# Half-height score matmuls in a two-layer hybrid kernel: 64 contracted rows per component instead of 128 with zeroed copies

## The reference, cut to what matters

```python
# branch A: a head's score is a 128-wide part plus a 64-wide rotary part (kr is shared by all heads)
sc = (einsum('bqhd,bkhd->bhqk', qn_b, kn) + einsum('bqhr,bkr->bhqk', qr_b, kr)) * scale   # 128 and 64 wide
# branch B: each head has two components (c = 0, 1) of width 64, with a softmax each
sc = einsum('bqhcd,bkhcd->bhcqk', q_b, k_b) * scale
p = softmax(where(mask, sc, -inf))
a = p[:, :, 0] - lam * p[:, :, 1]
# branch C: one 128-wide score per head, plus a bias
```

## Time and profile before

| | |
|---|---|
| median of 3 runs | 3480.88 us |
| the profiled execution | 3482.22 us |
| its span, first to last instruction | 3480.6 us |
| mean granted TensorE clock | 0.995 of full speed |
| matmul instructions | 28014 |
| DMA from and to memory | 584.18 MB, mean 168 GB/s |

### The profile page before, as it was taken

The page is one execution under the profiler, slowest core; times in us unless marked ns, Lnnn a source line. Parts: engine busy times, 40 slices in busy tenths (PEclk is TensorE's granted clock), DMA queues, the critical chain, the costliest instruction groups (busy, mean ns, idle before and its releaser), DMA issues. The chain is left out here.

```text
span 3480.6 us, 73373 instructions
## 1 busy us (share of the span) xinstructions
PE 3400.6 (98%) x28014; PEld 3325.1 (96%) x28014; DVE 2156.6 (62%) x3522; ACT 1701.2 (49%) x2781; POOL 184.6 (5%) x208
## 2 busy tenths in 40 slices
PE   7889999999999999999999999999999999999999
PEld 7888999999999998999999999999899999999999
DVE  6666756656656665667655665555667655565554
ACT  5444744434434454655544554444655554554443
POOL 1000000000000024000000100000000000000000
PEclk9999999999999999999999999999999999999999
DMA  4223555555555554344455445554344355444554
GB/s 178 97 96 115 174 181 187 195 184 183 192 181 193 184 178 155 134 151 151 149 195 185 177 156 187 187 188 172 131 152 152 142 180 200 174 160 181 182 188 169
DMA packets 90612, 584.18 MB, mean 168 GB/s; under 512 B 10480, under 2 KB 11120, under 8 KB 28400
## 3 DMA queue, kind: packets, MB, share of 16 engines
q1 hardware_dynamic: 88992, 577.60, 47.1%
q0 software_dynamic: 1488, 4.72, 0.4%
HBM read 580.19 MB, written 2.10 MB: 167 GB/s over the span
## 5 line engine op out<-in xcount | busy, mean ns | idle before, releaser
L185 PE MATMUL bank<-h,w_hi 128*128 128x256 f32 x5760 | 1640.2, 285 | 20.6 <-DVE w_lo L166 11.0
L166 DVE TENSOR_TENSOR w_lo<-raw,w_hi 128x768 fp32r<-128x768 f32 (+5 forms) x1202 | 1348.6, 1131 | 475.9 <-ACT w_hi L161 472.5
L186 PE MATMUL bank<-h,w_hi 128*128 128x256 f32 x5760 | 1611.6, 280 | 0.0
L187 PE MATMUL bank<-h,w_lo 128*128 128x256 f32 x5760 | 1610.1, 280 | 0.0
L161 ACT ACTIVATE w_hi<-raw 128x768 fp32r<-128x768 f32 (+5 forms) x1202 | 1105.8, 968 | 242.4 <-PE bank L187 225.9
L185 PEld LDWEIGHTS bank<-h,w_hi 128*128 128x128 f32 x5760 | 1086.1, 189 | 35.5 <-DVE w_lo L166 10.9
L186 PEld LDWEIGHTS bank<-h,w_hi 128*128 128x128 f32 x5760 | 1086.6, 189 | 2.8 <-issue 1.4
L187 PEld LDWEIGHTS bank<-h,w_lo 128*128 128x128 f32 x5760 | 1086.0, 189 | 0.0
L185 PE MATMUL bank<-mixed,w_hi 128*128 128x256 f32 x2368 | 666.4, 281 | 10.2 <-issue 5.8
L186 PE MATMUL bank<-mixed,w_hi 128*128 128x256 f32 x2368 | 663.4, 280 | 0.0
L187 PE MATMUL bank<-mixed,w_lo 128*128 128x256 f32 x2368 | 662.4, 280 | 0.0
(11 more groups left out here) (369 smaller groups left out, 2646.8 us busy)
## 6 DMA issues: line engine op xcount, KB each, us to landing
raw<-in_w SPq DMA_DIRECT2D x485, 1024.0 KB, 4.8
raw<-in_w_br SPq DMA_DIRECT2D x96, 512.0 KB, 4.2
raw<-in_w_uq SPq DMA_DIRECT2D x8, 768.0 KB, 4.3
raw<-in_w_ukv SPq DMA_DIRECT2D x8, 512.0 KB, 3.3
bias_t<-in_bias POOLq DMA_DIRECT2D x16, 192.0 KB, 3.2
x<-in_x SPq DMA_DIRECT2D x4, 512.0 KB, 7.9
raw<-in_w_kr SPq DMA_DIRECT2D x4, 512.0 KB, 3.3
out_x<-x SPq DMA_DIRECT2D x3, 512.0 KB, 7.8
```

Source lines behind the costliest of these rows:

```text
L166: dve.tensor_tensor(w_lo[:, b % 2, c], raw[:, b, c], w_hi[:, b % 2, c].bitcast(F32), ALU.subtract).then_inc(S["lo_done"], 1)
L185: pe.matmul(o, w_hi[:, b % 2, c], a_hi, start=start and k == t0, stop=False)
L186: pe.matmul(o, w_hi[:, b % 2, c], a_lo, start=False, stop=False)
L187: last = pe.matmul(o, w_lo[:, b % 2, c], a_hi, start=False, stop=stop and k == t0 + nt - 1)
```

## The change

The two half-empty copies go. The query of both components (branch B), and of both heads of a pair (branch A), lies in slot 0 alone, on its own half of the partitions. The score matmuls of branch B contract over 64 rows each, partitions 0 to 63 or 64 to 127, with the components alternating within a block: component 0 into `m[3]`, component 1 into `m[4]`, then the second block of each. The rotary matmul of branch A also contracts over the head's own 64 rows, between the 128-row matmuls of the first part. The POOL memset and its semaphore go; DVE's adds become one of 128 x 512 in `rotate` and one of 128 x 256 in `pair_rope`.

```diff
+HALVES = (slice(0, 64), slice(64, P))
...
-            pool.memset(qk[:, 0:2, :], 0.0).then_inc(S["qk_zero"], 1)
...
                 if br == BR_B:
-                    act.wait_ge(S["b_rope"], 3 * B)
+                    act.wait_ge(S["b_rope"], B)
...
-                for k, r in enumerate((slice(0, 64), slice(64, P))):
-                    dve.tensor_tensor(qk[r, k, :], rope[r, 0, :], rs[r, 0, :], ALU.add).then_inc(S["b_rope"], 1)
-                dve.tensor_tensor(qk[:, 2, :], rope[:, 1, :], rs[:, 1, :], ALU.add).then_inc(S["b_rope"], 1)
+                dve.tensor_tensor(qk[:, 0:3:2, :], rope, rs, ALU.add).then_inc(S["b_rope"], 1)
...
-                dve.wait_ge(S["qk_zero"], 1)
...
-                for k, r in enumerate((slice(0, 64), slice(64, P))):
-                    dve.tensor_tensor(qk[r, k, :], rope[r, 0, :], rope[r, 1, :], ALU.add).then_inc(S["qr_rope"], 1)
+                dve.tensor_tensor(qk[:, 0, :], rope[:, 0, :], rope[:, 1, :], ALU.add).then_inc(S["qr_rope"], 1)
...
-                    pe.wait_ge(S["b_rope"], 3 * B + 3)
+                    pe.wait_ge(S["b_rope"], B + 1)
                 else:
                     pe.wait_ge(S["qk_n"], 2 * T + 2)
-                for c in range(2 if br == BR_B else 1):
-                    q = qk[:, c if br == BR_B else 3, :]
+                if br == BR_B:
                     for k, (a, b) in enumerate(((0, P), (P, 3 * P))):
                         tok = slice(k * P, (k + 1) * P)
-                        mm = pe.matmul(m[3 + c][:, a:b], q[:, tok], qk[:, 2, 0:b - a], start=True, stop=br != BR_A)
-                        if br == BR_A:
-                            mm = pe.matmul(m[3 + c][:, a:b], qk[:, e, tok], kr[:, 0:b - a], start=False, stop=True)
-                    mm.then_inc(S[f"score{c}"], 1)
+                        for c, r in enumerate(HALVES):
+                            mm = pe.matmul(m[3 + c][:, a:b], qk[r, 0, tok], qk[r, 2, 0:b - a], start=True, stop=True)
+                            if k == 1:
+                                mm.then_inc(S[f"score{c}"], 1)
+                    return
+                r = HALVES[e]
+                for k, (a, b) in enumerate(((0, P), (P, 3 * P))):
+                    tok = slice(k * P, (k + 1) * P)
+                    mm = pe.matmul(m[3][:, a:b], qk[:, 3, tok], qk[:, 2, 0:b - a], start=True, stop=br != BR_A)
+                    if br == BR_A:
+                        mm = pe.matmul(m[3][:, a:b], qk[r, 0, tok], kr[r, 0:b - a], start=False, stop=True)
+                mm.then_inc(S["score0"], 1)
...
-                    pe.wait_ge(S["qr_rope"], 2 * pair + 2)
+                    pe.wait_ge(S["qr_rope"], pair + 1)
```

## The result

The changed kernel takes 3490.01 us (median of 18 runs, 3486.98 to 3502.4) against 3481.28 us (18 runs, 3477.05 to 3490.36): the ratio is 1.0028, with a 95% interval of 1.0019 to 1.0037. In a later comparison it took 3488.4 us (12 runs) against 3481.41, ratio 1.0014 (1.0006 to 1.0023). It is slower, by some 0.2%. The timed executions of both kernels fall into a faster group of 11 (3477 to 3483 before, 3486 to 3491 after) and a slower one of 7 (from 3485.6 and from 3495.0), and the medians of the two faster groups differ by 8.7 us as well.

A forecast was written before the change was run, and what follows sets the result against it. PE was taken to bound the kernel, busy 98% of the span. Terms +10.2 + 5.1 - 3.5 - 1.3 = +10.5 us on the median 3480.9 gave 3491.4 us; range 3478 to 3506, the forecast's own 3486 to 3497.

The forecast's parts named there:

- A trip into half height and back, 0.32: PE's score matmuls: going to half height and back costs 0.32 us, bounds 0 and 0.55.
- The hold: At a height change on PE, the weight load waits until the matmul ahead is nearly out: 0.206 or 0.31 us.
- the matmul follows its load by about 0.03: Going down to half height on PE, the matmul starts about 0.03 us after its load; going up, 0.10.
- Branch A, +10.2: Branch A's scores: two trips for each of 16 heads, 32 x 0.32 = +10.2 us, nothing overlapped, 0 absorbed.
- rival 4: Branch A's waits absorb their share: -6 us from the forecast, 3485.4 us; chance 0.08.
- Branch B's overlap, 0.22 a head: Branch B's score: neighbouring records on different halves overlap only at the long border, 0.22 us a head, -3.5 us.
- 0.44 that I gave as a bound: Branch B's score: at most the three borders between components overlap, 0.11 + 0.11 + 0.22 = 0.44 us a head.
- Branch B's trips, +5.1: Branch B's scores: one trip for each of 16 heads, 16 x 0.32 = +5.1 us.
- DVE's merged add, -1.3: Branch B: three adds become one, taking 0.65 us off PE's wait at each layer's first head, -1.3 us.
- Rival 1: PE's score matmuls: nothing held at 64 rows, trips 0, -1.3 to -4.8 us, some 3478 us; chance 0.14.
- rival 3: Score matmuls in both branches: halves run one behind the other, +21 to +32 us, taken at 3505; chance 0.18.
- Rival 2: Branch B's three borders: halves run side by side, trips cheap (below 0.17 us), -8.3 us, 3472.6; chance 0.08.

The follow-up runs named there:

- pe_a: Kernel before the change, with only branch A's rotary matmul cut to the head's own 64 rows: 3489.57 us against 3481.41, ratio 1.0024.
- a_grouped: Changed kernel with branch A's full-height blocks first, then its half-height rotary blocks: 3483.02 us against 3482.21, ratio 1.0006.
- pe_b_seq: pe_b with its loops exchanged, component 0 with both blocks and then component 1: one timed execution, 3480.73 us.
- best2: best1 with DVE's division of branch B's probabilities moved between the two parts of DVE's split: 3476.88 us (ratio 0.9992), then 3475.32 (0.9978).
- pe_b: Kernel before the change, with only branch B's score in half-height matmuls, components alternating; zeroed copies and three adds stay: 3480.21 us against 3481.41, ratio 0.9992.
- best1: Changed kernel with branch A as before, branch B as changed, in five slots: 3476.7 us (ratio 0.9989), then 3481.31 (0.9997).
- before_again: Kernel before the change, run once more without edit for its trace: one execution, 3477.81 us.
- after_again: Changed kernel, run once more without edit: 3488.4 us against 3481.41.

## Why the prediction was right, step by step

It said 3491.4 us and slower with a chance of 0.72; measured were 3490.0 and then 3488.4. The mechanism named, the price of changing the height, decides the sign: pe_a has it alone. But that the sum of +10.5 comes so near the measured +8.7 is luck: the trips were priced too low, the overlap in branch B much too low, and a wait that the prediction did not look for took some 2 us of the gain back. For branch B alone it had +0.3 (5.1 - 3.5 - 1.3), and measured was -3.0.

- *A trip into half height and back, 0.32.* Measured 0.40 (a_grouped: 6.4 us for 16). The hold was right, read from the 12-row product: the next load starts 0.20 us after a 128-column matmul and 0.31 after a 256-column one. Wrong was "the matmul follows its load by about 0.03" on the way down. With 64 rows it follows by 0.10, as on the way up. An A score should have taken 1.95 us by the prediction; it takes 1.31 + 0.78 = 2.09. The Trainium skill, TensorEngine Tiling (Array Packing), section Tiling Modes, says that changing the mode drains TensorE; the 64-row traces agree, with 0.20 each way.
- *Branch A, +10.2.* Measured +11.9 (pe_a): 16 x 0.78 less twice 0.35. That the waits at L2246 do not absorb it was right, and rival 4 fell with it; they stayed, 6.2 us before and 6.3 after. The "0 absorbed" was a little off all the same: the 0.29 a layer that PE had waited for DVE L1979 in the last pair (pe_a above) is gone.
- *Branch B's overlap, 0.22 a head.* This step failed. Measured 0.65, beyond even the 0.44 that I gave as a bound: 0.86 less the 0.20 of entering leaves 0.66 for eight records that took 1.31. I let only neighbours in program order overlap, and had weight loads of both halves share the 0.11 us spacing of the 12-row product. Both are refuted, the first by pe_b_seq, the second by the two loads at 2663.89. The page cited for this bound (the Trainium skill, TensorE: Matmul & The Clock Gate, Part 3) was the better guide: starts in different row groups a few ns apart, and loads that overlap. The trace has them 0.01 us apart. I had the rule and cut it down by a row of the 12-row product, which has one row group only.
- *Branch B's trips, +5.1.* Measured 16 x 0.40 = 6.4 (0.20 of entering, and 0.63 - 0.43 of leaving). With the overlap, PE's score gives 0.25 a head, 4.0 us in all; I had forecast a loss of 1.6.
- *Nothing late behind it.* This was not asked, and should have been: of the 0.25 a head, 0.19 went into waiting for DVE's probabilities in the loop's bodies. PE had only 0.08 us to spare there before. best2 moves DVE's step and gets it back.
- *DVE's merged add, -1.3.* Measured about -1.0: the wait went from 2.8 to 1.5 us, but pe_b's first heads gave part of it on their own. The add took 0.69, as L1945 had said. The adds of branch A gave nothing, as predicted: stretch A is +11.8 without them (after) and +11.9 with them (pe_a). For the memset no run stands alone.

Rival 1 (no change of mode) and rival 3 (halves one behind the other) fell. Rival 2 was half right: the halves do run fully side by side, but the trips are not cheap, 0.40 where it needed less than 0.17 (with its full overlap at 0.44; with 0.65 the point would lie at 0.24).

## What to carry to other kernels

Count the changes of contraction height, not only the rows: a half-height matmul inside full-height work costs a trip of 0.40 us here and saves nothing by itself, so a half-height part is best left at full height with zeros (best1), or else put at one end of its group, where it costs one trip instead of two (a_grouped). Half height pays where two independent halves run side by side and save more than that trip (0.65 us here). And where a step on the bound engine becomes shorter, look up how much it had to spare at its next operand: with 0.08 us to spare, three quarters of the gain of each head in the loop went into a wait, and moving the producer ahead of one long instruction returned it. The profile named no wait there, before or after. What gave it away was that the load kept the same 0.13 us to its producer's end while everything else had moved; and where nothing held it, in best2, it started 0.35 earlier.

## What the runs showed of the hardware that was not expected

- Matmuls on rows 0 to 63 and 64 to 127 with different PSUM tiles start within 0.01 us of each other, and TensorE finds such partners four records apart in program order (pe_b_seq: 0.86 us for the eight, as with alternating order).
- One and the same program ends the first block at 1302 or 1309 us (the two best2 traces: 1301.8 and 1309.4). The difference grows evenly over the long feed-forward part, where PE is busy without a break at a granted clock of 1.00 in both, but gets through 1% fewer matmuls in the same time (before, then after):

```profile
600.00:1000.00 400.00, 400.00 (x3431) 400.00 (x3431) 244.64 (x308) 171.92 (x213) 0.00 (x0) 1.00 0.56 189
600.00:1000.00 400.00, 400.00 (x3399) 400.00 (x3398) 244.50 (x306) 170.02 (x211) 0.00 (x0) 1.00 0.55 187
```

  Its cause stays open.
- Behind the 3.1 us in which PE stands still at the first block's end the clock is at 1.2 GHz in all traces, from PE's first record on or from at most 1 us later, for 6.1 us in before and 3.4 to 3.5 in before_again and after_again. Behind its 2.9 us at layer 0's start the clock fell for 3.1 us in before, 6.1 in after, and not at all in before_again and after_again. The two places together make up to 3.8 us between executions of one program (after and after_again).
